# A modulation vector's last sum moved from the tensor engine to DRAM and the vector engine, in a denoising trunk on one core

## The reference

```python
def adaln(cond, w, b):
    m = jax.nn.silu(cond) @ w + b            # w: (1024, 9 * 1024) per layer
    return [t[:, None, :] for t in jnp.split(m, N_MOD, axis=-1)]

def ffn_sublayer(x, shift, scale, gate, g_pre, g_post, w_in, w_out):
    h = modulate(rmsnorm(x, g_pre), shift, scale)
    a, b = jnp.split(h @ w_in, 2, axis=-1)
    h = (jax.nn.silu(a) * b) @ w_out
    return x + FFN_RES * gate * rmsnorm(h, g_post)
```

## Time and profile before

| | |
|---|---|
| median of 3 runs | 3024.62 us (3024.21 to 3026.36) |
| span of the profiled execution | 3023.0 us; the median lies 1.6 us above it |
| mean granted TensorE clock | 0.997 |
| PE busy | 2968.9 us (98%) |
| DVE busy | 2194.7 us (73%) |
| ACT busy | 1152.8 us (38%) |
| POOL busy | 594.5 us (20%) |
| DMA | mean 171 GB/s |

### The profile page before, as it was taken

The page is one execution under the profiler, slowest core; times in us unless marked ns, Lnnn a source line. Parts: engine busy times, 40 slices in busy tenths (PEclk is TensorE's granted clock), DMA queues, the critical chain, the costliest instruction groups (busy, mean ns, idle before and its releaser), DMA issues.

```text
span 3023.0 us, 46915 instructions
## 1 busy us (share of the span) xinstructions
PE 2968.9 (98%) x18458; PEld 2750.8 (91%) x18458; DVE 2194.7 (73%) x2831; ACT 1152.8 (38%) x1966; POOL 594.5 (20%) x586
## 2 busy tenths in 40 slices
PE   7999999999999999999999999999999999999999
PEld 6999888999999998999899999979999999888998
DVE  6888678887877656888887576768887888775444
ACT  4222664223322424222422365553224222664222
POOL 1111212112211212112211144541122112211001
PEclk9999999999999999999999999999999999999999
DMA  8667435665665445766566443337675766333443
GB/s 303 208 212 215 138 86 190 209 209 168 212 210 172 117 134 166 222 211 197 181 209 202 133 117 95 103 96 230 209 215 166 222 211 197 110 79 119 126 127 96
DMA packets 565935, 515.61 MB, mean 171 GB/s; under 512 B 43013, under 2 KB 499286, under 8 KB 563926
## 3 DMA queue, kind: packets, MB, share of 16 engines
q1 hardware_dynamic: 565158, 512.37, 55.7%
q10 hardware_dynamic: 560, 0.25, 0.0%
HBM read 509.31 MB, written 3.24 MB: 170 GB/s over the span
## 4 chain that ended last, share of the span: by engine, by line
PE 91%; issue 3%; DVE 2%; ACT 1%; POOL 1%; DMA 1%; SPq 0%; DVEq 0%; POOLq 0%; ACTq 0%
PE bank L1671 19%; PE bank L1673 19%; PE bank L1672 19%; PE bank L1720 9%; PE bank L1722 9%; PE bank L1721 9%; PE bank L1688 2%; PE bank L1695 1%; PE bank L614 1%; PE bank L639 1%; PE bank L1753 1%; DMA ada_first<-w_ada 1%; POOL small L2358 0%; POOL small L2363 0%; ACT tmp L1978 0%
## 5 line engine op out<-in xcount | busy, mean ns | idle before, releaser
L1671 PE MATMUL bank<-h_hi,w_hi 128*128 128x384 f32 x3328 | 1120.7, 337 | 0.0
L1673 PE MATMUL bank<-h_hi,w_lo 128*128 128x384 f32 x3328 | 1115.1, 335 | 0.0
L1672 PE MATMUL bank<-h_lo,w_hi 128*128 128x384 f32 x3328 | 1114.0, 335 | 0.0
L1925 ACT ACTIVATE w_hi<-raw 128x1024 fp32r<-128x1024 f32 x646 | 680.5, 1061 | 1030.9 <-PE bank L1673 478.2
L2081 DVE TENSOR_TENSOR w_lo<-raw,w_hi 128x1024 fp32r<-128x1024 f32 x648 | 812.2, 1277 | 328.5 <-ACT w_hi L1925 323.6
L2108 DVE SCALAR_TENSOR_TENSOR fold<-ada_raw,cond,fold 128x1024 f32<-128x1024 f32 x462 | 638.7, 1439 | 0.1
L1671 PEld LDWEIGHTS bank<-h_hi,w_hi 128*128 128x128 f32 x3328 | 625.5, 188 | 10.9 <-ACT tmp L1944 1.6
L1672 PEld LDWEIGHTS bank<-h_lo,w_hi 128*128 128x128 f32 x3328 | 625.4, 188 | 6.1
L1673 PEld LDWEIGHTS bank<-h_hi,w_lo 128*128 128x128 f32 x3328 | 625.3, 188 | 0.0
L2399 POOL TENSOR_TENSOR h_lo<-tmp,h_hi 128x384 fp32r<-128x384 f32 x176 | 280.4, 1593 | 1737.6 <-DVE h_hi L2142 1737.6
L1720 PE MATMUL bank<-w_hi,h_hi 128*128 128x512 f32 x1056 | 415.4, 393 | 0.0
(11 more groups left out here) (204 smaller groups left out, 2422.4 us busy)
## 6 DMA issues: line engine op xcount, KB each, us to landing
raw<-w_ffn_in SPq DMA_DIRECT2D x352, 512.0 KB, 5.0
ada_raw<-w_ada SPq DMA_DIRECT2D x264, 512.0 KB, 4.2
raw<-w_ffn_out SPq DMA_DIRECT2D x176, 512.0 KB, 4.6
raw<-w_hgrn_in SPq DMA_DIRECT2D x40, 512.0 KB, 4.0
g_rows<-g_dram SPq DMA_DIRECT2D x12, 1024.0 KB, 6.7
raw<-w_attn_qkv SPq DMA_DIRECT2D x24, 512.0 KB, 6.1
raw<-w_conv_in SPq DMA_DIRECT2D x24, 512.0 KB, 4.9
ada_first<-w_ada SPq DMA_DIRECT2D x16, 512.0 KB, 11.7
```

The lines of the kernel that those rows point to most:

```text
L1671: mm(out, wh, h_hi[:, k, :], start=(k == 0), stop=False)
L1672: mm(out, wh, h_lo[:, k, :], start=False, stop=False)
L1673: last = mm(out, wl, h_hi[:, k, :], start=False, stop=(k == DC - 1))
L1925: A(w_hi[:, b % RING, :], raw[:, b % RAW, :], ACT.Copy).then_inc(w_hi_made, 1)
```

## The change

The sum over the four groups of 32 partitions, the bias and the column form are made without PE. `fold_sum` writes its result in another order and in two halves, one per group of the modulation. SP writes these sums (32 KB) to a DRAM tensor, `write_sums`, and reads them back with four DMAs, `spread_sums`, so that each partition gets the four partial sums of its own channels (128 pieces of 64 B in each DMA). Then DVE adds the four and the bias in `mod_fold`, two rounds after the sum (at f = 21 for the sum of f = 20). On SP the write stands behind the load of block `at_a(f) + 11` and the spread behind the load after it, both cut to the last block of the sub-layer.

```diff
-    def folds_of(s):
-        return {f + 1: u for f, u in sums_of(s).items()}
+    def mods_of(s):
+        return {min(f + 2, FC - 1): u for f, u in sums_of(s).items()}
+
+    def spreads_of(s):
+        last = 3 * FC - 1
+        return {min(at_a(f) + 11, last): u for f, u in sums_of(s).items()}
...
+        def write_sums(u):
+            sp.wait_ge(sums_made, 2 * sum_number[u])
+            sp.dma_start(fold_dram[u], fold_sums[:, :, :, :].rearrange("p r g c -> p r (g c)")).then_inc(fold_written, 16)
+
+        def spread_sums(u):
+            sp.wait_ge(fold_written, 16 * sum_number[u])
+            sp.wait_ge(mods_made, u)
+            for r in range(4):
+                sp.dma_start(fold_parts[32 * r:32 * r + 32, :, :, :].rearrange("i a g c -> i a (g c)"),
+                             fold_dram[u, :, r, :].rearrange("(a i) x -> i a x", a=4)).then_inc(fold_spread, 16)
...
                 if sub_kind[s] == "ffn":
                     if b == n_blocks(s) - 3:
                         write_gains(s)
+                    if b - 1 in writes:
+                        spread_sums(writes[b - 1])
+                    if b in writes:
+                        write_sums(writes[b])
+                        if b == n_blocks(s) - 1:
+                            spread_sums(writes[b])
...
-        def fold_columns(u, bank):
-            pe.wait_ge(sums_made, sum_number[u])
-            need(pe, mods_made, u)
-            parts = fold_sums[:, :, :].rearrange("p g (c r) -> p r c g", r=4)
-            for r in range(4):
-                out = psum[bank][32 * r:32 * r + 32, T:T + 2 * DC].rearrange("p (c g) -> p c g", g=2)
-                last = mm(out, quad, parts[:, r], start=True, stop=True, tile_position=(0, 32 * r))
-            last.then_inc(ada_turned, 1)
...
-                if f in folds:
-                    pe.wait_ge(a_read, n0 + f + 1)
-                    fold_columns(folds[f], 6)
                 if 1 <= f <= FC - TAIL:
                     out_block(s, f - 1, b0 + at_o(f - 1))
-                if f in folds and f < FC - 1:
-                    pe.wait_ge(mods_made, folds[f] + 1)
...
-            V.tensor_reduce(fold_sums[:, :, :], fold[:, :, :].rearrange("p g (b i) -> p g b i", i=32), AX_X, ALU.add,
-                            apply_transpose=True).then_inc(sums_made, 1)
+            need(dve, fold_written, 16 * (sum_number[u] - 1))
+            for g in range(2):
+                V.tensor_reduce(fold_sums[:, :, g, :], fold[:, g, :].rearrange("p (c r i) -> p r c i", r=4, i=32), AX_X,
+                                ALU.add, apply_transpose=True).then_inc(sums_made, 1)
+
+        def mod_fold(u):
+            dve.wait_ge(fold_spread, 4 * 16 * sum_number[u])
+            V.tensor_reduce(mod[:, mod_cols(u), :].rearrange("p c g -> p g c"),
+                            fold_parts[:, :, :, :].rearrange("p a g c -> p g c a"), AX_X, ALU.add).then_inc(fold_added, 1)
+            dve.wait_ge(fold_added, sum_number[u])
             bias = b_cols[:, mod_cols(u)].unsqueeze(2).to_broadcast([P, DC, 2])
+            V.tensor_tensor(mod[:, mod_cols(u), :], mod[:, mod_cols(u), :], bias, ALU.add).then_inc(mods_made, 1)
```

More of the change, by code:

```diff
@@ L79, in host_constants @@
         masks[:, lv] = ((kb % 2 == 0) & (qb == kb + 1)) | ((qb % 2 == 0) & (kb == qb + 1))
-    quad = np.zeros((P, 32), np.float32)
-    quad[m, m % 32] = 1.0
-    base = np.concatenate([ident, sel, quad], axis=1).astype(np.float32)
+    base = np.concatenate([ident, sel], axis=1).astype(np.float32)
     return {"k_base": base, "k_attn": np.ascontiguousarray(attn), "k_masks": masks.reshape(P, -1)}
@@ L210, in build @@
     direct_units = [1, 0]
-    def turned_ahead(u):
-        return direct_units.index(u) if u < 2 else u
     for s in range(N_SUB):
@@ L281, in build @@
     fold = place("fold", [P, 2, D], F32, x_end - 2 * D * 4)
-    fold_sums = place("fold_sums", [P, 2, D // 32], F32, x_end - 2 * D * 4 - 2 * D // 32 * 4)
+    fold_sums = place("fold_sums", [P, 4, 2, DC], F32, x_end - 2 * D * 4 - 2 * D // 32 * 4)
+    fold_parts = place("fold_parts", [P, 4, 2, DC], F32, x_end - 2 * D * 4 - 2 * (2 * D // 32 * 4))
     span_rest = (span[0] + 7 * D * 4, x_end)
@@ L290, in build @@
     ada_rows = place("ada_rows", [P, ADA_COLS], F32)
-    base_k = place("base_k", [P, P + 40], F32)
-    ident, sel, quad = base_k[:, 0:P], base_k[:, P:P + 8], base_k[:, P + 8:P + 40]
+    base_k = place("base_k", [P, P + 8], F32)
+    ident, sel = base_k[:, 0:P], base_k[:, P:P + 8]
     ones = place("ones", [P, P], F32)
@@ L307, in build @@
     g_dram = nc.dram_tensor("g_dram", [N_SUB, 2, DC, P], F32, kind="Internal").ap()
+    fold_dram = nc.dram_tensor("fold_dram", [DEPTH * N_MOD, P, 4, 2 * DC], F32, kind="Internal").ap()
     psum_stack = ExitStack()
@@ L323, in build @@
     fold_made, sums_made = sem("fold_made"), sem("sums_made")
+    fold_written, fold_spread, fold_added = sem("fold_written"), sem("fold_spread"), sem("fold_added")
     ada_used, rows_copied, rows_made = sem("ada_used"), sem("rows_copied"), sem("rows_made")
@@ L490, in sp_core_start @@
             a = attn_number(s)
-            sp.wait_ge(sums_made, sum_number[units_end[s - 1] - 1])
+            sp.wait_ge(sums_made, 2 * sum_number[units_end[s - 1] - 1])
             sp.dma_start(attn_k[:, :], ins["k_attn"]).then_inc(attn_in, 16)
@@ L1589, in sub_layer @@
             slabs = {}
+            writes = spreads_of(s) if sub_kind[s] == "ffn" else {}
             if sub_kind[s] == "ffn":
@@ L1779, in out_tail @@
                     pe.wait_ge(b_read, FC * (ffn_number(s) + 1))
-                    need(pe, mods_made, units_end[s])
                 pe.wait_ge(hf_low, NT * e + 1)
@@ L1823, in ffn @@
             b0, n0 = first_block[s], FC * ffn_number(s)
-            folds = folds_of(s)
             for f in range(FC):
@@ L1930, in ada_copy @@
             act.wait_ge(ada_used, 2 * direct_units.index(u) + 1)
-            need(act, ada_turned, turned_ahead(u))
+            need(act, ada_turned, direct_units.index(u))
             A(ada_rows[:, :], psum[bank][:, 0:ADA_COLS], ACT.Copy).then_inc(rows_copied, 1)
@@ L2100, in fold_slab @@
             if k == 0:
-                need(dve, sums_made, sum_number[u] - 1)
+                need(dve, sums_made, 2 * (sum_number[u] - 1))
             for g in range(2):
@@ L2113, in fold_sum, with mod_add @@
             dve.wait_ge(fold_made, fold_number[u, DC - 1])
-            need(dve, ada_turned, u)
-            V.tensor_reduce(fold_sums[:, :, :], fold[:, :, :].rearrange("p g (b i) -> p g b i", i=32), AX_X, ALU.add,
-                            apply_transpose=True).then_inc(sums_made, 1)
-        def mod_add(u, bank, at=0):
-            dve.wait_ge(ada_turned, turned_ahead(u) + 1)
-            bias = b_cols[:, mod_cols(u)].unsqueeze(2).to_broadcast([P, DC, 2])
-            V.tensor_tensor(mod[:, mod_cols(u), :], psum[bank][:, at:at + 2 * DC].rearrange("p (c g) -> p c g", g=2),
+            need(dve, fold_written, 16 * (sum_number[u] - 1))
[7 more added lines that the diff above has]
+            dve.wait_ge(fold_added, sum_number[u])
+            bias = b_cols[:, mod_cols(u)].unsqueeze(2).to_broadcast([P, DC, 2])
+            V.tensor_tensor(mod[:, mod_cols(u), :], mod[:, mod_cols(u), :], bias, ALU.add).then_inc(mods_made, 1)
+        def mod_add(u, bank):
+            dve.wait_ge(ada_turned, direct_units.index(u) + 1)
+            bias = b_cols[:, mod_cols(u)].unsqueeze(2).to_broadcast([P, DC, 2])
+            V.tensor_tensor(mod[:, mod_cols(u), :], psum[bank][:, 0:2 * DC].rearrange("p (c g) -> p c g", g=2),
                             bias, ALU.add).then_inc(mods_made, 1)
@@ L2126, in ffn @@
             b0, n0 = first_block[s], FC * ffn_number(s)
-            sums, folds = sums_of(s), folds_of(s)
+            sums, mods = sums_of(s), mods_of(s)
             split_to = 6
@@ L2142, in ffn @@
                 V.tensor_copy(h2_hi[:, f % H2, :], tmp[:, 2 + f % 2, :]).then_inc(h2_hi_made, 1)
-                if f in folds:
-                    mod_add(folds[f], 6, T)
+                if f in mods:
+                    mod_fold(mods[f])
                 if f in sums:
```

## The result

| | before | after |
|---|---|---|
| median of the runs | 3024.41 us (3023.92 to 3026.36, 4) | 3051.55 us (3049.42 to 3053.42, 4) |
| span of the profiled execution | 3023.0 us | 3047.6 us |
| mean granted TensorE clock | 0.997 | 0.991 |
| ratio after to before | | 1.0084, 95% interval 1.0072 to 1.0096 |

The change makes the kernel slower. The forecast was 3058 us (3040 to 3075). The profiled execution after has the shortest span of the four; the others are 1.5 to 4.0 us longer, at mean clocks of 0.989 to 0.990.

What follows compares the result with a forecast made beforehand. PE was taken as the bound, busy 2968.9 of 3023.0 us. Less 12.9 us of foldings, plus 38 of stands and 8.5 of clock, the span became 3056.6 and the median, 1.6 above the span, 3058 us (3040 to 3075).

Steps and rivals of the forecast that it cites:

- The gain: On the PE queue: 33 foldings of 0.39 us go away, 12.9 us saved if nothing else becomes late.
- Mid-FFN units: 28 of 33 units inside FFNs: new DVE work and the spread hide, DVE having 1.52 us idle before L2138.
- the bias addition: On DVE, 16 columns wide: 0.17 us like the old one, some 0.5 us with the four-element reduction and a semaphore.
- The five ends: Ends of FFN sub-layers 0, 2, 5, 8, 9: PE idles (stands) 7.6 us for late block 66, 38 us in all.
- Step 2: At an FFN end, the sums' write lands: 2.5 us plus 0.1 wake-up; high bound 4.7, if written as 512 pieces.
- 3, four spreads and the gains: On SP at an FFN end: four spread issues at 0.43 us each, then 0.37 for the gains' read.
- step 4: At an FFN end, block 66 lands 7.0 us after its issue, between bounds 6.1 and 9.0.
- 5, both splits, product, low part: After block 66 lands: ACT split 1.06, DVE split 1.23, product through POOL's low part 2.04, hand-over 0.1 us.
- The clock: At each of five stands, PE's granted clock falls once, losing 1.7 us of work; 8.5 us in all, bounds 0 and 8.5.
- The rival with the stand but no fall: At the five FFN ends: PE stands but its clock doesn't fall, 3050 us; chance 0.15.
- Sum: Whole kernel: 3023.0 - 12.9 + 38 + 8.5 = 3056.6 us of profiled span, 3058 us as median of runs.
- half of the way from 38 to 67 us: Upper end of the range: high bounds of the five stands half used, taken as 17 us, 3058 + 17 = 3075.

Runs made afterwards that it cites:

- kernel 1: Changed kernel, but SP issues the gains and the next sub-layer's first two blocks before the last trip of an FFN: 3012.04 us, ratio 0.995.
- kernel 6: Changed kernel, but PE folds the five units with f = 20 as before, the other 28 going through DRAM: 3014.4 us, ratio 0.9961.
- kernel 7: Kernel 1 with DVE's add of the four parts and bias add moved ahead of the copy to h2_hi: 3010.36 us, ratio 0.9952.
- kernel 3: Changed kernel with the gains read issued ahead of the last write of the sums: 3035.1 us, ratio 1.0028.
- kernel 8: Kernel 1 with AHEAD = 1, so only block 66 goes ahead of the write and block 67 follows the spreads: 3011.7 us, ratio 0.9957.
- kernel 11: Kernel 4 with the gains read issued in front of SP's added wait: 3033.59 us, ratio 1.003.
- kernel 5: Changed kernel with 24 unused matmuls on PE before its wait for chunk 21's low part at the five ends: 3044.11 us, ratio 1.0065.
- kernel 4: Kernel before, foldings on PE, with only SP's wait for the f = 20 sum added ahead of gains and block 66: 3045.03 us, ratio 1.0063.
- kernel 2: Changed kernel with DVE's split of block 66 at f = 21 moved behind its product: 3045.01 us, ratio 1.0057.
- kernel 10: Kernels 2 and 3 together on the changed kernel, gains read first and DVE's split after its product: 3021.43 us, ratio 0.9987.

## Why the prediction was right, point by point

**The gain (12.9 us).** Right. The step from L1695 to L1743 is 737.72 - 737.31 = 0.41 us, also where a folding used to lie. Without stands, kernel 1 is 0.5% below before, where 12.9 us are 0.43%.

**Mid-FFN units (hidden).** Right, by kernels 1 and 6 and by DVE, which never waits for the spread. The two half reductions take 2.36 us against 2.30. The load of block 24 goes out at 112.67 (forecast 112.5), and ACT splits it unhindered at 118.74. Wrong was the size of the bias addition: 0.92 us in 33 places, where I took the 0.17 of a like one with an operand in PSUM. Then the new work on DVE is 0.26 + 0.92 = 1.2 us, not 0.5, still under the 1.52 us of idle time; and most of it was not new work but the wait for POOL, which its neighbour bore before (kernel 7).

**The five ends (7.6 us each; measured 6.0, and 6.47 in sub-layer 2).** The mechanism was right in each step. Against the sum's end at 733.00 us in the trace after:

| step | forecast | measured |
|---|---|---|
| 2, write until the spreads can go | 2.6 us | 2.4 (733.00 to 735.41) |
| 3, four spreads and the gains | 2.1 | 2.3 (to 737.68) |
| 4, block 66 lands | 7.0 | 6.2 (to 743.85) |
| 5, both splits, product, low part | 4.4 | 4.4 (to 748.24) |

The largest miss is step 4, a term a little too large. I took 7.0, between the 9.0 and the 6.1 of the earlier trace rows, with something for the 512 pieces of the spreads in front. But the 6.1 is itself a load right behind the gains, with nothing older in flight, as this view of the kernel before shows (KB, us to landing; first there, from 431.8 us, then after, from 737.2 us):

```profile
g_rows<-g_dram SPq DMA_DIRECT2D x1, 1024.0 KB, 4.3
raw<-w_ffn_in SPq DMA_DIRECT2D x1, 512.0 KB, 6.1
...
g_rows<-g_dram SPq DMA_DIRECT2D x1, 1024.0 KB, 4.7
raw<-w_ffn_in SPq DMA_DIRECT2D x1, 512.0 KB, 6.1
```

So the right row was at hand, and the pieces of the spreads added nothing to it. What the forecast had no row for is a load without gains in front: by kernels 3, 8 and 11 it is there 3.9 to 4.2 us after its issue, and 6.2 to 6.5 with them. The other four ends stand 0 to 1.1 us shorter than sub-layer 2.

Step 2 was right in size, but its high bound came from a write of 512 pieces, and this one was not that. Between 733.0 and 735.4 us, where nothing but the write is under way on the queue, the trace after has 144 packets in all:

```profile
q1 hardware_dynamic: 144, 0.03, 7.3%
```

32 KB in so few packets are pieces of over 200 B on average. The Trainium skill (DMA: Bandwidth & Descriptors, "Anatomy of one DMA") puts 2.0 us of fixed cost on a DMA of the GpSimd path; the write with its semaphore took 2.4 us here on a quiet queue, the median of all such writes is 4.4. So the trace agrees on the quiet queue, and beside other loads the write took longer.

**The clock (8.5 us).** The mechanism was right, a fall at each of the five ends; the size was too small. Behind the five stands 11.2 us were lost, 2.2 an end and not 1.7, and kernel 5 gives 10.4 of them back. In the span only 7.7 of rest arrive, since other places are 3.5 us shorter than before; that the total comes so near to 8.5 is partly luck. The rival with the stand but no fall, at 3050, came nearer in time than the forecast, but only because the stands were 8.2 us smaller than forecast; its mechanism is refuted. The shape was another than in the earlier trace rows: the clock falls during the stand or at its end and then holds 0.50 for 3.4 to 5.6 us of work, where the row had one stretch of 3 us and a little more.

**Sum.** The profiled span was forecast at 3056.6 and is 3047.6. Of the 9.0 us, 8.2 are the stands (38 - 29.8). The other 0.8 is the difference of two misses: 2.7 us more for the clock at the ends, 3.5 less elsewhere. One sum in the range was off: half of the way from 38 to 67 us is 14.5 and not 17, so the upper end would have been 3072; it decides nothing here.

**What the forecast left out:** that the wait for the sum alone is half of the stand (kernel 4). I priced the trip step by step, and the removal of any one step would have looked like a repair; but the late block reaches PE by two ways, DVE's split ahead of the product and ACT's split ahead of the squares (kernel 2). An earlier load of block 66 closes both (kernels 1 and 8); the two partial repairs together left 1.6 us an end (kernel 10).

## What to carry to other kernels

A queue that waits for something holds back all that stands behind it, so put a trip of small transfers behind the loads that the next stage needs first, even if its own result is then later: here one moved trip turned +0.84% into -0.5%, and the traffic was free. Before moving a wait away from one reader of a late buffer, list its other readers: ACT's in-order queue took over where DVE's was relieved. And look at the size of what is issued just ahead of an urgent load, not only at its issue time: 1024 KB in front cost 2.0 to 2.5 us of landing.

## What the runs showed of the hardware

- DVE and POOL don't work on SBUF side by side in these forms. In the changed kernel a DVE addition of 16 columns with both operands in SBUF ends with POOL's low part (DVE, then POOL):

```profile
119.90 0.92 DVE L2130 TENSOR_TENSOR mod<-mod,b_cols 128x16 f32<-128x16 f32 x1
...
119.77 1.02 POOL L2413 TENSOR_TENSOR h_lo<-tmp,h_hi 128x384 fp32r<-128x384 f32 x1 [10.48 <-DVE h_hi L2156]
```

  It took 0.175 us without POOL at work (kernel 7), where POOL's own instruction then met DVE's next one and took 1.98 us instead of 1.02. The Trainium skill says it so (SBUF — State Buffer, "SBUF: two separate sides"): the port pair that the two share is an exclusive lock, which a DVE instruction with two SBUF inputs needs against a GpSimd one that reads SBUF, and the later one blocks. The trace agrees, and the forecast should have used it.
- The granted clock fell to 0.50 at all five stands of 5.4 to 6.5 us, in sub-layer 2 already before PE went on. At the five stands of 2.6 to 3.1 us of kernel 4 it fell behind two and stayed at 1.00 behind three. 5.3 us of matmuls whose results nobody reads kept it at 1.00 in sub-layer 2 (kernel 5).
- The landing of the 32 KB store (144 packets) took from 1.5 to 5.6 us, beside the loads of the other blocks; 2.4 us on a quiet queue.
